# Moving the two split-weight tiles by whole allocations in a two-block transformer kernel, so that they begin at byte 64 modulo 512

## The reference, cut to what matters

```python
# first block
u_ctx = modulate(ctx, csh1, csc1) @ w_in[l]
u_lat = modulate(x, sh1, sc1) @ w_in[l]
...
x = post_norm(x, mix_lat, g1, ln1_g[l], ln1_b[l])
ffn_lat = conv_ffn(modulate(x, sh2, sc2), ffn_w_up[l], ffn_conv_w[l], ffn_conv_b[l], ffn_w_down[l], True)
x = post_norm(x, ffn_lat, g2, ln2_g[l], ln2_b[l])
# second block, two layers: attention with selected keys, mLSTM, an FFN of width 4096, a gate
h = x
for i in range(DEPTH_2):
    h = hybrid_layer(h, p[i], cos, sin, g_mix[i], w_in[i], ...)
```

## The kernel before, in words

| tile | bytes | begins at | modulo 512 |
|---|---|---|---|
| small | 4096 | 13888 | 64 |
| turn | 432, rounded to 448 | 17984 | 64 |
| h | 16384 | 18432 | 0 |
| xh | 16384 | 34816 | 0 |
| xl | 16384 | 51200 | 0 |
| wh | 16384 | 67584 | 0 |
| wl | 16384 | 83968 | 0 |
| mix | 16384 | 100352 | 0 |
| ring | 16384 | 116736 | 0 |
| arenas and `acts`, one over the other | | 133120, `acts` of the two layers 145408 and 178176 | 0 |
| ctxr | 16384 | 198080 | 448 |

## Time and profile before

### The profile page before, as it was taken

One profiled execution on the slowest core, in us unless ns is written; L12 is line 12 of the kernel. 1 busy time (PEld: TensorE's weight loads), 2 busy tenths in 40 slices (PEclk: granted clock), 3 DMA queues, 4 the chain that ended last, 5 costly groups with the idle time before them and its releaser, 6 DMA issues.

```text
span 2057.3 us, 26250 instructions
## 1 busy us (share of the span) xinstructions
PE 2013.4 (98%) x10148; PEld 1574.5 (77%) x10148; DVE 1135.5 (55%) x2020; ACT 867.9 (42%) x1381; POOL 917.4 (45%) x1157
## 2 busy tenths in 40 slices
PE   6999999999999999999999999999999999999998
PEld 2877676888888767768888888786776788888877
DVE  5366758988393579955522231466996543222235
ACT  4542434443233556784322222445578532222242
POOL 1344205876566325541555555302355155555540
PEclk9999999999999999999999999999999999999999
DMA  9034631322323211103333323322111332332331
GB/s 328 25 108 143 217 123 50 105 94 80 121 84 102 89 42 42 62 21 123 92 103 103 99 86 103 102 69 83 42 42 42 103 97 98 103 103 83 102 102 62
DMA packets 188299, 194.26 MB, mean 94 GB/s; under 512 B 8592, under 2 KB 184080, under 8 KB 187792
## 3 DMA queue, kind: packets, MB, share of 16 engines
q1 hardware_dynamic: 187600, 189.44, 28.5%
q10 hardware_dynamic: 576, 3.15, 0.4%
HBM read 190.48 MB, written 2.10 MB: 94 GB/s over the span
## 4 chain that ended last, share of the span: by engine, by line
PE 88%; DVE 6%; POOL 2%; ACT 2%; DMA 1%; issue 1%; SPq 0%; DVEq 0%; ACTq 0%; POOLq 0%
PE ps L808 20%; PE ps L810 20%; PE ps L809 20%; PE ps L827 3%; PE ps L829 3%; PE ps L828 3%; PE ps L855 2%; POOL wl L2900 1%; DVE mix L2512 1%; PE ps L844 1%; PE ps L845 1%; PE ps L846 1%; PE ps L1355 1%; PE ps L1428 1%; PE ps L1411 1%; PE ps L1374 1%
## 5 line engine op out<-in xcount | busy, mean ns | idle before, releaser
L2900 POOL TENSOR_TENSOR wl<-ring,wh 128x256 fp32r<-128x256 f32 x1008 | 754.2, 783 | 807.5 <-ACT wh L1465 807.2
L1465 ACT ACTIVATE wh<-ring 128x1024 fp32r<-128x1024 f32 (+1 forms) x298 | 309.0, 1044 | 311.1 <-PE ps L810 256.9
L808 PE MATMUL ps<-xh,wh 128*128 128x512 f32 (+1 forms) x976 | 383.1, 393 | 2.6 <-POOL wl L2900 2.6
L810 PE MATMUL ps<-xh,wl 128*128 128x512 f32 (+1 forms) x976 | 380.6, 390 | 0.0
L809 PE MATMUL ps<-xl,wh 128*128 128x512 f32 (+1 forms) x976 | 380.6, 390 | 0.0
L808 PE MATMUL ps<-acts,wh 128*128 128x512 f32 x880 | 343.5, 390 | 0.7 <-POOL wl L2900 0.4
L810 PE MATMUL ps<-acts,wl 128*128 128x512 f32 x880 | 342.4, 389 | 0.0
L809 PE MATMUL ps<-acts,wh 128*128 128x512 f32 x880 | 342.4, 389 | 0.0
L2512 DVE SCALAR_TENSOR_TENSOR mix<-ps,par,mix 128x441 f32<-128x441 f32 (+2 forms) x352 | 213.7, 687 | 29.3 <-ACT mix L1712 29.3
L808 PEld LDWEIGHTS ps<-xh,wh 128*128 128x128 f32 (+1 forms) x976 | 183.0, 188 | 47.0 <-issue 9.1
L810 PEld LDWEIGHTS ps<-xh,wl 128*128 128x128 f32 (+1 forms) x976 | 183.0, 187 | 39.4
(11 more groups left out here) (443 smaller groups left out, 3031.4 us busy)
## 6 DMA issues: line engine op xcount, KB each, us to landing
ring<-in_w_ff_dram SPq DMA_DIRECT2D x64, 1024.0 KB, 5.2
ring<-in_w_in_dram SPq DMA_DIRECT2D x28, 1024.0 KB, 5.0
ring<-in_ffn_w_up_dram SPq DMA_DIRECT2D x22, 1024.0 KB, 4.9
ring<-in_w_ada_dram SPq DMA_DIRECT2D x17, 1024.0 KB, 5.0
ring<-in_w_out_dram SPq DMA_DIRECT2D x12, 1024.0 KB, 5.1
ring<-in_ffn_w_down_dram SPq DMA_DIRECT2D x8, 1024.0 KB, 5.0
ring<-in_w_ple_gate_dram SPq DMA_DIRECT2D x8, 1024.0 KB, 5.0
early<-in_w_ada_dram SPq DMA_DIRECT2D x7, 1024.0 KB, 10.8
```

Of the source, the lines that this page charges most:

```text
L808: t.matmul(b[0:m, 0:n], s.hi[:, k, a:a + m], x2[0][:, k, :], start=k == ks[0], stop=False)
L810: i = t.matmul(b[0:m, 0:n], s.lo[:, k, a:a + m], x2[0][:, k, :], start=False, stop=k == ks[-1])
L1465: a.activation(s.hi[:, :, c], s.ap[:, :, c], ACT.Copy).then_inc(*up("hi", "hi", name, hf))
L2900: i = p.tensor_tensor(s.lo[:, k:k + 2, c], s.ap[:, k:k + 2, c], s.hi[:, k:k + 2, c].bitcast(F32), ALU.subtract)
```

## The change

The line that allocates `wh` and `wl` moves ahead of the one that allocates `turn`, the tile of 108 float32 whose 448 bytes bring the tiles behind it to a multiple of 512.

```diff
         rope, eps, csil_t, small = sb("rope", 64), sb("eps", 3), sb("csil", 256), sb("small", 1024)
+        wh_t, wl_t = sb("wh", 2 * SLOT, F32R), sb("wl", 2 * SLOT, F32R)
         turn_t = sb("turn", 108)
         h_t, xh_t, xl_t = sb("h", 4096), sb("xh", 4096, F32R), sb("xl", 4096, F32R)
-        wh_t, wl_t = sb("wh", 2 * SLOT, F32R), sb("wl", 2 * SLOT, F32R)
         mix_t, ring = sb("mix", 4096), sb("ring", NSLOT * SLOT)
```

## The result

The changed kernel takes 2097.4 us (median of 4 runs, 2096.2 to 2099.2) against 2059.2 us before (4 runs, one more than in the table of the kernel before, 2056.9 to 2059.8): ratio 1.0187, 95% interval 1.0172 to 1.0201. It is 1.9% slower, where 2045 us and a range of 2024 to 2092 were forecast.

The account below looks back on a forecast made before the run. PE's matmul pace was taken as the bound. From a 2057.3 us span, 14.5 us came off for the 512-column matmuls, the other terms being nothing: 2042.8, plus 2.1 for the median, forecast 2045 us, range 2024 to 2092.

Parts of the forecast that it names:

- What bounds the kernel: Whole kernel: PE is the bound, busy 98% of the span, its waits small; only the pace of matmul streams matters.
- The count: In `product`: 6576 float32r matmuls of 512 columns, 1491 us at 226.7 ns each, 72% of the span.
- the first term of the sum: 512-column matmuls with stationary `wh`, `wl`: moving them to 64 saves 2.2 ns on each of 6576, 14.5 us.
- The inference from `ctxr` to an address: 256-column streams: context product at 117.8 ns against `product_t` at 120.0, the 2.2 ns put down to `ctxr` beginning at 448.
- The transfer across the number of columns: The 2.2 ns seen at 256 columns was applied unchanged to 512, since the surplus was 12.5 and 12 ns.
- The upper bound of that term: 512-column matmuls: streams don't settle and stay at 232.9 ns, 6.2 ns more on each of 6576, 41 us more.
- the second rival: 512-column stream settles worse, at 229 to 233 ns: 14 to 41 us more, 2074 to 2100 us; chance 30%.
- The range: Whole kernel: 2024 to 2092 us, given 82%, taking in two thirds of the settles-worse case's 30%.
- The second term: 960 matmuls of 256 columns with weights moving (`product_t`): taken as nothing, bounds 9.6 us less to 6.0 us more.
- The third: 144 matmuls with `ctxr` moving, offset becoming 128 bytes: taken as nothing, bounds -1.1 to +0.3 us.
- The fourth: Engines writing `wh`, `wl`: any slowdown, even 10% on POOL's 754 us, stays hidden under PE; nothing added.
- The rule of a separate port: Opposing skill rule: TensorE loads weights through an independent read port, so their address can't slow the moving stream; sum 2059.4.

Follow-up runs that it names:

- e7: Kernel before, tiles unmoved, with `product` making each block of 512 columns as two passes of 256-column matmuls: 2127.0 us.
- e8: Kernel before with `product` splitting each 512-column block into two of 256, and `wh` and `wl` moved to 64 modulo 512: 2098.4 us.
- e1: Against the kernel before, `turn` allocated behind `wh`, `wl`, so `h`, `xh`, `xl`, `wh`, `wl` all begin at 64 modulo 512, `acts` at 0: 2075.9 us.
- e2: Against the kernel before, only `xh` and `xl` moved to begin at 64 modulo 512; `wh`, `wl` and `acts` stay at 0: 2063.2 us.
- e4: Against the kernel before, `wh` and `wl` allocated earlier, to begin at 256 modulo 512, all moving tiles at 0: 2058.4 us.
- e13: Kernel before, tiles unmoved, with `product` using 64 stationary columns instead of 128 for all but the first and last k: 2070.6 us.

## Why the prediction was wrong, point by point

**What bounds the kernel** was right: PE waits as much as before, and the span grew by what its pitch grew. **The count** of 6576 matmuls was right: they give +40.0 us, of which 1.4 are the clock, and `product_t` and the rest take the net to 38.7.

**The step that failed is the first term of the sum**, "It was seen at 256 columns, but the surplus is the same at 256 and 512 (12.5 and 12 ns), so I use it unchanged." The sign was wrong: +6.5 ns with `acts` and +6.0 with `xh` moving instead of -2.2. The surplus was indeed equal at offset 0: taken over half of the pitch at half clock (213.3 and 106.7 ns, an estimate of the pace without surplus), it is 13.3 ns for either number of columns. That did not mean that it is equal at 64: e7 and e8 show the same move giving -3 to -4 ns at 256 columns, and e1 +6.5 ns at 512. The inference from `ctxr` to an address was right in sign for 256 columns (the splitting kernels and e2 bear it out), though its 2.2 ns was no fixed price: the same move gave 3.1 to 3.8 ns in `product`. The transfer across the number of columns was only argued.

**The upper bound of that term was right**: "the streams don't settle and stay at the 232.9 ns of the earlier trace rows" gives +41 us, 2100 us, and the measured 233.3 ns and 2097.4 us lie 0.4 ns above and 3 us below. That they lie so near is in part luck: the row that the bound comes from, with 80 stationary columns, went from 232.7 to 230.2 ns under the same change. This was the second rival, given 30%, with every unsettled row of 512 columns on its side and one row of another form against. Its picture, that the pitch of before is a place into which the stream must fall, fits the curve: of the ten places tried, 0 and 256 alone reach 226.7 to 226.8 with `acts`, and four end at 233.3. But that the changed stream doesn't settle was wrong: it does, into a pattern of 231 and 236.

**The range** cut this rival's band at 2092 although its own bound reached 2100.

**The second term** was taken as nothing: `product_t` gained 2.0 to 2.2 ns, about 2 us, and with the clock 2.6 us in all, within its bounds (-9.6 to +6.0 us). The offset there is the opposite one, and at 256 columns it too is better than 0. **The third** (`ctxr`) was nothing: 17.1 and 17.2 us. **The fourth** was right: ACT and POOL kept their lengths, and all moves by whole multiples of 512 changed nothing (in e4 `xh` lies 32768 bytes further up and the pitch is that of before).

**The rule of a separate port.** The changed trace contradicts what the sum would be by it: moving the weights alone by 64 bytes slowed the moving stream by 6.0 to 6.5 ns per matmul, and e1 shows that it depends on how the two operands lie to each other. The Trainium skill, page SBUF — State Buffer, section "A bandwidth-pool intuition that's wrong (but worth ruling out)", gives the weight loads a second, independent read port; for this stream of float32r at full clock the measurement decides against independence, and says nothing of where the two meet. The 216 ns for 512 columns that the prediction takes from the Trainium skill, page TensorE: Matmul & The Clock Gate, section "Back-to-back issue gap", are given there for a matmul by itself and not for a stream with its loads, so they could not tell whether there was a surplus to win.

**What stays open** is the mechanism inside. Shown are the cause (how the two operands begin to each other; that only the remainder modulo 256 counts rests on two pairs), that the price isn't per byte of load, and that at half clock the offset costs nothing. That the reads of the two operands collide fits all this, but is argued, not seen. The settled pitch isn't a function of offset and columns alone either: in e7 the context tokens' stream (`ctxr`, offset 64) runs at 114 ns, where the kernel before has 117.8 for the same instructions at the same addresses; what came before it in the queue differs. And at the same offset of 64 the products with `acts` step 231 and 236 ns in turn in the changed kernel but 233 or 234 every time in e1, with the same mean.

## What to carry to other kernels

Where PE is the bound and streams float32r with hardly a pause, look where the stationary and the moving tile begin modulo 256 bytes, before tiles are reordered for another reason: moving one allocation, which changed no instruction, cost 1.9% here. Measure it at the number of moving columns that the kernel has, since the offset of 64 was a gain at 256 columns and a loss at 512. And a stream's cost from a row of another shape belongs into the bounds, not into the forecast, as long as a row of the right number of columns says something else.

## What the runs showed of the hardware that was not expected

- The pitch of 512-column float32r matmuls with `acts` moving is 226.8 ns at offsets 0 and 256, 228.9 at 192 and 448, 232.4 at 128, 233.3 at 32, 64, 160 and 480, 234.3 at 352. With 256 columns `product` has 120.0 at offset 0 (e7) and 116.2 to 116.9 at 64 (e8).
- At half clock the offset costs nothing: 426 or 427 ns for 512 columns and 213 or 214 for 256 in nearly every step, in all runs; the cost of the offset shows at full clock alone.
- Loading 64 stationary columns instead of 128 made the stream slower, 230.0 against 226.8 ns, at offset 0 (e13).
- Plain float32 matmuls stayed at 592 ns of length in both kernels.
